# Feed-forward of a two-model kernel on Trainium2: gate, up and down as seven products of half blocks in place of eight

## The chip, the cores and the metric

The kernel runs on one core of a Trainium2 chip. The metric is the device time of one execution in microseconds (us); the median of three runs is given. The engines are TensorE (PE, with its weight loads shown as PEld), VectorE (DVE), ScalarE (ACT), GpSimd (POOL) and SyncE (SP), which issues every DMA of this kernel from one queue in program order.

## The reference, cut to what matters

The kernel computes a block with attention branches and a feed-forward, and then a second model of two layers. The change is in the first block's feed-forward alone. x1 is 1024 tokens by 1024 features, D_FF is 2816:

```python
h2 = rms_norm(x, norm_ffn[l])
x = x + (jax.nn.silu(h2 @ w_ffn_gate[l]) * (h2 @ w_ffn_up[l])) @ w_ffn_down[l]
```

Everything is float32. Each operand of a product is split into a high part (rounded to the type that TensorE takes) and a low part (the rest), and each product is three matmuls: high by high, high by low, low by high.

## The kernel before, in words

`build` first writes one list, `work`, of operations; then each engine walks the whole list in order and does what is its own. So the order in which the helpers emit operations is the order of every engine's queue. Each instruction waits for semaphores with `wait_ge`; an engine that waits holds all that stands behind.

PSUM has eight banks of 128x512. `DB` hands out six in turn for products, `TB` two (5 and 6) for the transposes of rows (`row_T`). A `Place` is one use of a bank: its `before` is that the last use has been read, `full` that the matmuls are done, `read` that it has been read. The operations that matter:

- `mm3` (L2108): for each block of 128 in the contracted dimension three matmuls of 128x128 by 128x512; before them it waits for `place.before`, for the weights' split and for its operands.
- `w_split` (L2209 on ACT makes the high part, L2371 on DVE the low part): weights come from DRAM in chunks of 1 MB into two raw buffers and are split into two double buffers.
- `row_T` (L2114, L2218, L2448): PE transposes four blocks of 128x128 into a bank of TB, ACT writes the high part, DVE the low part and frees the bank.
- `row_sq` (L2213, ACT), two short GpSimd operations (L2692, L2695) and `row_scale` (L2443, DVE): the norm of a tile of 128 rows.

The stage before the feed-forward, `row_tiles`, makes x1 from the output projection: for rows t = 0 to 3, then 4 to 7, first the left then the right half of the columns. After each product of a right half the generator `norm_row(t)` is queued, and each `tick()` moves all queued generators one step: square, scale, transpose.

The feed-forward runs over 22 strips of 128 hidden features in parts of 2, 4, 4, 4, 4 and 4 strips (`FFN_PARTS`). `f_half` makes one strip for half of the tokens:

```python
mm3(r.gate, r.gate.ps[:, :], views(ch.part(0), slice(0, 128)), views(hpair, cut), 8, ch.split, h_at[4 * hf + 3])
tick()
r.up = DB.take()
m = mm3(r.up, r.up.ps[:, :], views(ch.part(1), slice(0, 128)), views(hpair, cut), 8, ch.split)
...
emit("silu", r)
```

`silu` is a tanh on ACT (L2303), a multiply each with the gate and up banks on DVE (L2584, L2587), and the split of the strip (L2307 on ACT, L2590 on DVE). After each part the down product adds its strips: for each of two halves of the columns and each of eight row tiles one `mm3` over the part's strips, and one DVE addition into x1 in SBUF (L2579). The strips never leave SBUF. The last part goes through `row_tiles` again with `x2_row`, which stores the finished row to DRAM and transposes it for the second model's first products, one row per tick. These `row_T` write with a stride (`unmix`). GpSimd has no work of size in the stage.

Of the kernel before, what the change touches and what calls it, by code (L numbers as in the profile page):

```python
# [36 lines left out]
FFN_PARTS = (2, 4, 4, 4, 4, 4)  # L37
# [4 lines left out]
def weight_plan():  # L42
# [39 lines left out]
    f0 = 0  # L82
    for nf in FFN_PARTS:
        for f in range(f0, f0 + nf):
            add(("w_ffn_gate", 0, 8, [(f * 128, 128)]), ("w_ffn_up", 0, 8, [(f * 128, 128)]))
        for c in range(2):
            add(("w_ffn_down", f0 * 128, nf, [(512 * c, 512)]))
        f0 += nf
# [24 lines left out]
    return plan, extra  # L113
# [96 lines left out]
def build(nc, d):  # L210
    plan, extra = weight_plan()
# [6 lines left out]
    with ctx:  # L218
# [80 lines left out]
        w_todo, w_eager = [], [False]  # L299

        def w_load():
            i = ws["loaded"]
            if i >= len(plan):
# [11 lines left out]
        def w_split():  # L315
            i = ws["split"]
            if i >= len(plan) or (i in extra and not extra_bufs[extra[i]]):
                return
# [25 lines left out]
            if w_eager[0]:  # L344
                w_pump(i)

# [62 lines left out]
        def mm3(place, out, lhs, rhs, nk, split, *operands, last=True, blocks=None, start=True, stop=True):  # L409
# [7 lines left out]
            r.split, r.operands = split, flat(*operands)  # L417
            emit("mm3", r)
            w_pump()
            return place.full  # L420
# [38 lines left out]
        def row_T(src, t, ready, dst=None, unmix=False):  # L459
# [7 lines left out]
            for q0 in range(0, nk, 4):  # L467
# [4 lines left out]
                r.hi_done = signal("turned_hi")  # L472
# [858 lines left out]
        t_x1 = {t: load(f"xb{t}", x1[:, t, :], mixed_rows(d["x"], t), osp, gm["branch"]) for t in range(8)}  # L1331
# [9 lines left out]
        def row_tiles(chunks, lhs, blocks, add, finish, by_block=False, eager=True, first=False):  # L1341
# [22 lines left out]
            for t0 in (0, 4):  # L1364
                for j in range(2):
# [22 lines left out]
                    if t0:  # L1388
                        for ch in chs():
                            ch.done(m)  # L1390
            w_eager[0] = False
# [17 lines left out]
        xsf = [rest(f"xsf{i}", [T], F, (36 + 4 * i) * KB) for i in range(2)]  # L1409
        sqf = rest("sqf", [T], F, 44 * KB)  # L1410
        t_gbf = load("gbf", gbf[:, :], d["norm_ffn_b"], mix_read)
        x1_done, h_at = dict(t_x1), {}
        xsf_free = [None, None]

        def norm_row(t):
            r = Rec()
            r.src, r.junk, r.ss, r.n, r.loaded = x1[:, t, :], sqf[:, :], stat(1), T, flat(x1_done[t], mix_read)
            row_sq(r)
            yield
            r.out, r.gain, r.free = xsf[t % 2][:, :], gbf[:, :], flat(t_gbf, xsf_free[t % 2])  # L1420
            row_scale(r)
            yield
            p = row_T(xsf[t % 2][:, :], t, r.scaled)
            h_at[t], xsf_free[t % 2] = p.read, p.full

        x_last = row_tiles(chunks, lambda t: views(hpair, sl(t * 128, 128)),
                           lambda t: [(k, mix_rows[k, t // 4]) for k in range(8)], add_rows("x1"), norm_row, True)

        strips = Slots([(rest(f"fhi{i}", [T], R, 8 * i * KB), rest(f"flo{i}", [T], R, (8 * i + 4) * KB)) for i in range(6)])
        for i in range(4):  # L1430
            strips.free[i] = [x_last]

        def f_half(ch, strip, f_free, hf, made):

            fh, fl = strip
            r = Rec()
            cut = slice(hf * 512, hf * 512 + 512)
            r.gate = DB.take()
            mm3(r.gate, r.gate.ps[:, :], views(ch.part(0), slice(0, 128)), views(hpair, cut), 8, ch.split, h_at[4 * hf + 3])
            tick()  # L1440
            r.up = DB.take()
            m = mm3(r.up, r.up.ps[:, :], views(ch.part(1), slice(0, 128)), views(hpair, cut), 8, ch.split)
            tick()
            r.f_free = f_free
            r.si, r.t, r.t_free = scr.take()
            r.tanh, r.hi_done, r.lo_done = signal("f_tanh"), signal("f_hi"), signal("f_lo")
            r.hi, r.lo = fh[:, cut], fl[:, cut]
            emit("silu", r)
            scr.free[r.si] = [r.lo_done]
            made.append(r.lo_done)  # L1450
            return m

        f0 = 0
        for nf in FFN_PARTS:
            got = []
            if f0 == 0:
                chs, taken, made = [Chunk(), Chunk()], [strips.take(), strips.take()], [[], []]
                for hf in range(2):
                    for f in range(2):
                        m2 = f_half(chs[f], taken[f][1], taken[f][2], hf, made[f])  # L1460
                        if hf:
                            chs[f].done(m2)
                got = [(taken[f][0], *taken[f][1], made[f]) for f in range(2)]
                for i in range(4, 6):
                    strips.free[i] = flat(h_at[7], xsf_free)
            else:
                for f in range(nf):
                    ch = Chunk()
                    fi, pair, f_free = strips.take()
                    made = []  # L1470
                    for hf in range(2):
                        m2 = f_half(ch, pair, f_free, hf, made)
                    ch.done(m2)
                    got.append((fi, *pair, made))
            last_h = m2
            lhs_h, lhs_l = [g[1] for g in got], [g[2] for g in got]

            def rows_of(t):
                cut, hs_, ls_ = sl(t * 128, 128), lhs_h, lhs_l
                return (lambda k: hs_[k][:, cut]), (lambda k: ls_[k][:, cut])  # L1480

            def strips_of(t, got=got):
                return [(k, g[3][t // 4]) for k, g in enumerate(got)]

            f0 += nf
            if f0 < 22:
                add = add_rows("ffn")
                for c in range(2):
                    ch = Chunk()
                    for t in range(8):  # L1490
                        p = DB.take()
                        m = mm3(p, p.ps[:, :], rows_of(t), views(ch.part(0), slice(0, 512)), nf, ch.split, blocks=strips_of(t))
                        add(t, c, p)
                    ch.done(m)
                for g in got:
                    strips.free[g[0]] = [m]
                if f0 == 18:
                    m2r = rest("m2r", [8, 256], F, 32 * KB)
                    t_m2 = load("mem2", m2r[:, :, :], d["mem2T"], m)
                continue  # L1500

            x2_st, x2_last = {}, {}

            def x2_row(t):
                x2_st[t] = store("x2", mixed_rows(d["x2"], t), x1[:, t, :], x1_done[t])
                yield
                p = row_T(x1[:, t, :], t, x1_done[t], unmix=True)
                h_at[t], x2_last[t] = p.read, p.full

            m2l = rest("m2l", [8, 256], R, 32 * KB)  # L1510
            m2h = rest("m2h", [8, 256], R, 40 * KB)
            m2_hi, m2_lo = signal("m2_hi"), signal("m2_lo")
            emit("m2_split")
            pairs_ = [[Chunk()], [Chunk()]]
            m = row_tiles([lambda: pairs_[0], lambda: pairs_[1]], rows_of, strips_of, add_rows("ffn"), x2_row)
        ffn_done = m
# [6 lines left out]
        def x2_free():  # L1523
            return flat(x2_st[7], list(x2_last.values()))

        for l in range(2):
            ch = Chunk()
            for s in range(2):
# [3 lines left out]
                evac(p, [(kv[l][:, 0, s, :], p.ps[:, 0:256])], x2_free())  # L1532
# [22 lines left out]
        scr_free = flat(scr.free)  # L1555
# [356 lines left out]
        t_rx2 = {t: load(f"x2b{t}", x1b[:, t, :], d["x2"][t * 128:(t + 1) * 128, :], x2_free(), c_dead) for t in range(8)}  # L1912
# [140 lines left out]
        def h1_back(t, *dead):  # L2053
            t_rh1[t] = load(f"h1b{t}", x1b[:, t, :], d["h1"][:, t, :], h1_st[7], mem_dead, *dead)
# [17 lines left out]
        while pend:  # L2072
# [3 lines left out]
                                                   ("out", "h1", "x2", "kv1", "outB"))] + t_outC + t_outA  # L2076
# [20 lines left out]
        def _(e):  # L2097
            w = Waits(e, None)

            def mm3_run(r):  # L2100
# [3 lines left out]
                for k, made in r.blocks:  # L2104
                    if made:
                        w.wait_ge(*made)
                    for a, b in ((lh(k), rh(k)), (lh(k), rl(k)), (ll(k), rh(k))):
                        x = e.matmul(r.out, a, b, start=(r.start and m == 0), stop=(r.stop and m == n - 1))  # L2108
# [8 lines left out]
            for kind, r in work:  # L2117
                if kind == "mm3":
# [4 lines left out]
                    if r.last:  # L2123
                        x.then_inc(r.place.full[0], 1)
                elif kind == "row_T":
# [76 lines left out]
        def _(e):  # L2202
            w = Waits(e, semaphore("act_step"))
            for kind, r in work:
# [9 lines left out]
                elif kind == "row_T":  # L2214
                    w.wait_ge(*w.last)
                    w.wait_ge(*r.place.full)
                    pv = r.place.ps[:, 0:r.nb * 128].rearrange("p (k c) -> p k c", k=r.nb)
# [569 lines left out]
```

## Time and profile before

| | before |
|---|---|
| median of 3 runs (lowest, highest) | 3192.62 us (3191.34, 3193.46) |
| span of the profiled execution | 3191.1 us; the profile gives no other time for it, the runs' median is 1.5 us above its span |
| PE, DVE, ACT, POOL busy in the span | 99%, 47%, 38%, 18% |
| feed-forward stage | about 1500 to 2220 us of the span |
| mean granted clock of PE | 0.998 |

How to read it: a busy share is the time in which at least one instruction of the engine ran. A matmul's row shows its whole passage (0.39 us for 128x512), which overlaps the next one; distances between starts tell how fast they go. A granted clock of 1.00 is TensorE's 2.4 GHz, 0.50 is 1.2 GHz. "x2" in a row is two instructions in a row whose time is given together; brackets hold the idle time before and what ended it.

### The profile page before, as it was taken

What the parts mean: (1) busy time and instruction counts of PE and PEld (TensorE: products, weight loads), DVE (VectorE), ACT (ScalarE), POOL (GpSimd) and SP (SyncE); (2) the same over time, 40 slices, a digit from 0 to 9 for tenths busy, and PEclk for the clock granted to TensorE, in tenths of its full rate; (3) what the DMA queues carried; (4) which work ended last, traced back from release to release, by engine and by line L of the source; (5) the groups of instructions that cost most, each with busy time, mean ns of one, the idle gap of its engine ahead of it and who ended that gap; (6) DMA issues with size and microseconds to landing.
All of it is one profiled execution on the core that took longest, in us unless ns stands there. A gap on an engine that the chain in (4) does not pass through costs nothing.

```text
span 3191.1 us, 49353 instructions
## 1 busy us (share of the span) xinstructions
PE 3143.4 (99%) x18948; PEld 2674.9 (84%) x18948; DVE 1513.3 (47%) x3186; ACT 1215.6 (38%) x2410; POOL 565.1 (18%) x818
## 2 busy tenths in 40 slices
PE   7999999999999999999999999999999999999999
PEld 7988889999999888888888888888977777687777
DVE  6657673343354233344432333335344565753775
ACT  5446565444444122132111121124433555622452
POOL 3423334353450000000000000000101110022141
PEclk9999999999999999999999999999999999999999
DMA  5010101111113121130111111113210000212012
GB/s 202 34 47 21 34 21 47 48 54 51 44 51 103 51 75 50 50 139 14 66 42 52 53 40 53 53 53 111 77 36 27 15 28 14 97 57 89 27 60 100
DMA packets 48315, 182.44 MB, mean 57 GB/s; under 512 B 14480, under 2 KB 18704, under 8 KB 35280
## 3 DMA queue, kind: packets, MB, share of 16 engines
q1 hardware_dynamic: 48080, 179.28, 16.2%
q8 instruction: 151, 2.47, 0.3%
q14 instruction: 84, 0.69, 0.1%
HBM read 159.54 MB, written 19.46 MB: 56 GB/s over the span
## 4 chain that ended last, share of the span: by engine, by line
PE 94%; DVE 3%; ACT 2%; issue 1%; DMA 0%; POOL 0%; DVEq 0%; SPq 0%; POOLq 0%; ACTq 0%
PE ps L2108 75%; PE ps L2148 7%; PE ps L2156 3%; PE ps L2114 2%; PE ps L2163 2%; PE ps L2179 2%; PE ps L2171 1%; PE ps L2182 1%; PE ps L2199 1%; DVE wlo L2371 0%; DVE qk L2479 0%; DVE xsc L2443 0%; DVE mPT L2524 0%; DVE mE L2493 0%; DMA min<-in_mem 0%
## 5 line engine op out<-in xcount | busy, mean ns | idle before, releaser
L2108 PE MATMUL ps<-hhi,whi 128*128 128x512 f32 x1568 | 616.4, 393 | 0.0
L2108 PE MATMUL ps<-hhi,wlo 128*128 128x512 f32 x1568 | 610.9, 390 | 0.0
L2108 PE MATMUL ps<-hlo,whi 128*128 128x512 f32 x1568 | 610.1, 389 | 0.0
L2108 PE MATMUL ps<-whi,hhi 128*128 128x256 f32 (+2 forms) x1920 | 580.4, 302 | 1.3 <-DVE hlo L2573 0.9
L2108 PE MATMUL ps<-whi,hlo 128*128 128x256 f32 (+2 forms) x1920 | 563.7, 294 | 0.0
L2108 PE MATMUL ps<-wlo,hhi 128*128 128x256 f32 (+2 forms) x1920 | 563.5, 293 | 0.0
L2692 POOL TENSOR_SCALAR stats<-stats 128x2 f32<-128x2 f32 (+2 forms) x230 | 60.4, 263 | 1937.9 <-ACT jk L2213 805.0
L2108 PEld LDWEIGHTS ps<-whi,hhi 128*128 128x128 f32 x1920 | 368.3, 192 | 10.9 <-issue 3.2
L2108 PEld LDWEIGHTS ps<-wlo,hhi 128*128 128x128 f32 x1920 | 368.8, 192 | 7.6 <-issue 0.2
L2108 PEld LDWEIGHTS ps<-whi,hlo 128*128 128x128 f32 x1920 | 368.3, 192 | 7.7
L2108 PEld LDWEIGHTS ps<-hhi,wlo 128*128 128x128 f32 x1568 | 294.3, 188 | 62.1
L2108 PEld LDWEIGHTS ps<-hhi,whi 128*128 128x128 f32 x1568 | 294.5, 188 | 59.6 <-issue 0.7
L2108 PEld LDWEIGHTS ps<-hlo,whi 128*128 128x128 f32 x1568 | 294.6, 188 | 59.2
L2209 ACT ACTIVATE whi<-raw 128x1024 fp32r<-128x1024 f32 (+2 forms) x154 | 150.8, 979 | 291.8 <-PE ps L2108 286.9
L2371 DVE TENSOR_TENSOR wlo<-raw,whi 128x1024 fp32r<-128x1024 f32 (+2 forms) x154 | 173.0, 1123 | 166.7 <-ACT whi L2209 164.2
L2685 POOL CAST whi<-raw 128x512 fp32r<-128x512 f32 (+4 forms) x172 | 108.7, 632 | 649.9 <-PE ps L2108 640.5
L2687 POOL TENSOR_TENSOR wlo<-raw,whi 128x512 fp32r<-128x512 f32 (+4 forms) x172 | 219.2, 1274 | 13.8
L2695 POOL TENSOR_TENSOR stats<-stats 128x2 f32<-128x2 f32 (+2 forms) x230 | 165.6, 720 | 19.2
L2579 DVE TENSOR_TENSOR x<-ps,x 128x512 f32<-128x512 f32 x112 | 77.4, 691 | 160.5 <-PE ps L2108 159.5
L2108 PE MATMUL ps<-whi,fhi 128*128 128x512 f32 x352 | 137.5, 391 | 0.0
L2108 PE MATMUL ps<-whi,flo 128*128 128x512 f32 x352 | 137.0, 389 | 0.0
L2108 PE MATMUL ps<-wlo,fhi 128*128 128x512 f32 x352 | 136.9, 389 | 0.0
(351 smaller groups left out, 5198.5 us busy)
## 6 DMA issues: line engine op xcount, KB each, us to landing
raw<-in_W SPq DMA_DIRECT2D x93, 1024.0 KB, 4.9
raw<-in_W SPq DMA_DIRECT2D x24, 768.0 KB, 4.4
orw<-scratch_outs SPq DMA_DIRECT2D x6, 1024.0 KB, 5.4
xin<-in_x SPq DMA_DIRECT2D x8, 512.0 KB, 10.9
bW<-scratch_bw SPq DMA_DIRECT2D x8, 512.0 KB, 3.7
x<-in_x SPq DMA_DIRECT2D x8, 512.0 KB, 7.3
scratch_x<-x SPq DMA_DIRECT2D x8, 512.0 KB, 3.7
x1b<-scratch_x SPq DMA_DIRECT2D x8, 512.0 KB, 7.4
```

The source lines that it names most:

```text
L2108: x = e.matmul(r.out, a, b, start=(r.start and m == 0), stop=(r.stop and m == n - 1))
L2114: x = e.transpose(place.ps[0:rows, j * 128:(j + 1) * 128], b, ident[:, :])
L2148: x = e.matmul(p.place.ps[:, o:o + n], *p.blocks[b], start=True, stop=True)
L2156: x = e.transpose(r.place.ps[0:n, j * 128:(j + 1) * 128], r.u.E[:, o:o + n], ident[:, :])
L2163: x = e.matmul(r.v_place.ps[:, 0:r.ew], r.PT[:, j * 128:(j + 1) * 128], r.V[j], start=(j == 0), stop=(j == r.nblk - 1))
L2179: x = e.matmul(r.v_place.ps[64 * s:64 * s + 64, 0:128], u.V[j], u.PT[:, j * 128:(j + 1) * 128], start=(j == 0), stop=(j == r.nblk - 1))
L2209: e.activation(r.hi, r.raw, ACT.Copy).then_inc(w.sig(r.hi_done), 1)
L2371: e.tensor_tensor(r.lo, src, r.hi.bitcast(F), ALU.subtract).then_inc(w.sig(r.lo_done), 1)
L2579: e.tensor_tensor(r.o, r.place.ps[:, :], r.o, ALU.add).then_inc(w.sig(r.place.read), 1)
L2685: e.tensor_copy(r.hi, r.raw).then_inc(w.inner(), 1)
L2687: e.tensor_tensor(r.lo, r.raw, r.hi.bitcast(F), ALU.subtract).then_inc(w.sig(r.lo_done), 1)
L2695: e.tensor_tensor(r.ss, r.ss, half_neg[:, 0:n], ALU.pow).then_inc(w.sig(r.rstd), 1)
```

## The change: what it does

All three products become products of 2x2 blocks made with seven block products and sums of blocks (Winograd's form), where the plain form has eight.

- **Gate and up.** Activations h are cut into feature halves by token halves. Products use b11 (features low, tokens early), b21, b22 and the sums t1 to t4. The norm's late rows therefore make differences and sums with the early rows (DVE `combine`) and transpose five groups of four blocks. The weights of strips k and k + 11 with gate and up each give four half blocks of 128x512; `WeightSet` loads them (1 MB), makes four sums on GpSimd and splits seven operands on ACT and DVE. There are two sets; while one strip is computed, the next is loaded, summed and split.
- **Each of 22 strips** is seven products of 12 matmuls in the order p1, p6, p2, p7, p5, p4, p3 over four banks; p2, p4 and p3 continue a bank that an earlier product filled and that has been read in between (`joined`).
- **Finished strips.** After each odd strip GpSimd makes four sums of the outputs, and seven blocks per pair are stored to DRAM (`fs`).
- **Down** runs at the end as seven products of 11 steps; a step reads one stored strip (256 KB) and one weight block (256 KB), splits both (sums of weight blocks on GpSimd in products 2 to 5), and does 12 matmuls into four banks, three to a bank. Each product's banks are added to 1 to 4 targets of x1 (`down_add`). x1 itself is stored to DRAM before the norm and read back.
- The other weight stream is held back (`held`) from the output projection to step 40 of down. x2 rows 4 to 7 are finished during the last product, rows 0 to 3 after it, all four in the same ticks.

The diff, cut to its core:

```diff
+FF_PAIRS = 11
+FF_FIRST = ("b11", "b21", "b22", "t4", "t1", "t2", "t3")
+FF_WEIGHT = (0, 1, 6, 3, 4, 5, 2)
+FF_DOWN = ((0, "11", (0, 1, 2, 3)), (1, "21", (0,)), (4, "t1", (1, 3)), (2, "t3", (2, 3)), (5, "t2", (1, 2, 3)),
+           (3, "t4", (2,)), (6, "22", (1,)))
...
+            def load(self, i):
+                free = flat(self.raw_free() if i < 2 else self.done[:4])
+                self.landed = load(f"wf{self.x}", self.raw4[:, :, :], d["WF"][i], free)
+            def sums(self, i):
+                free = [flat(self.sums_free()) if i < 2 else flat(self.done[j]) for j in (4, 5, 6)]
+                a11, a12, a21, a22, s1, s2, s4 = self.raw
+                sum1 = combine(True, s1, a21, a22, ALU.add, self.landed, free[0])
+                sum3 = combine(True, a21, a11, a21, ALU.subtract)
+                sum2 = combine(True, s2, s1, a11, ALU.subtract, free[1])
+                sum4 = combine(True, s4, a12, s2, ALU.subtract, free[2])
+                self.ready = [self.landed, self.landed, sum3, self.landed, sum1, sum2, sum4]
+                self.after = [sum2, sum4, sum3, sum1, sum2, sum4, sum4]
...
+            # norm_row, rows 4 to 7
+            one = combine(False, h_diff[u % 2][:, :], xs[:, early], x0[:, early], ALU.subtract, hd_free[u % 2])
+            three = combine(False, xs[:, early], xs[:, late], xs[:, early], ALU.subtract)
             yield
+            p = row_T(xs[:, late], t, r.scaled, [w[:, 4:8, :] for w in hpair])
+            q = row_T(h_diff[u % 2][:, :], t, one)
+            s = row_T(xs[:, early], u, three, (t3h, t3l))
+            two = combine(False, x0[:, early], xs[:, early], x0[:, early], ALU.add, row_full[u])
+            four = combine(False, x0[:, late], x0[:, late], x0[:, early], ALU.subtract)
...
+            def keep(self):   # after p1, on ACT
+                evac(self.m1, [(self.x, self.m1.ps[:, :])], fX_free[self.i % 2])
+            def p6(self):
+                p = product(self.i, 6, self.b.take())
+                ff_add(self.x, p, self.x)
+            def u3(self):
+                ff_add(fU, self.m7, self.x)
+            def c22(self):
+                ff_add(fU, self.m5, fU)
+            def c21(self):
+                ff_add(fV, self.m4, self.x)
+                ff_out(self.i, 0, fV)
+            def p3(self):
+                self.m3 = product(self.i, 3, self.d.take(), joined=True)
+            def end(self):
+                i, k = self.i, self.i // 2
+                c12 = ff_add(self.x, self.m3, self.x)
+                fX_free[i % 2] = ff_gate(1, self.x, c12)
+                ff_out(i, 1, fU)
+                if i % 2 == 0:
+                    fo_free[0] = [fs_store(0, k, fo_made[0])]
+                    return
+                # four combine(True, ...) on GpSimd, then six stores:
+                #   fs_store(1), (3), (4, sum1), (2, sum3), (5, sum2), (6, sum4)
...
+        for i in range(2, last_strip + 1):
+            s, here, other = Strips(i), sets[i % 2], sets[1 - i % 2]
+            more = i < last_strip
+            if more:
+                other.load(i + 1)
+                other.sums(i + 1)
+            s.p1()
+            s.keep()
+            here.split(i, 6)
+            s.p6()
+            s.p2()
+            s.p7()
+            s.gate_early()
+            s.p5()
+            s.u3()
+            if more:
+                other.split(i + 1, 0, 5)
+            s.p4()
+            s.c22()
+            if more:
+                other.split(i + 1, 1, 2)
+            s.p3()
+            s.c21()
+            if more:
+                other.split(i + 1, 4, 3)
+            s.end()
...
+        for s, (p, k) in enumerate(steps):
+            strip_load(s + 4)
+            down_load()
+            if s % 3 and x1_order:
+                x1_back(x1_order.pop(0))
+            prepare(s + 2)
+            if k == 0:
+                places = [bank[4 * (p % 2) + n].take() for n in range(4)]
+            # four mm3 of one block each, then:
+            if before and k < 4:
+                down_add(p - 1, before, k)
+            if s == 40:
+                w_release(f1_last)
+            if s in (50, 56):
+                w_split()
...
+        for n in range(4):
+            down_add(6, before, n)
+            pend.append(x2_row(n))
+        tick()
```

On DVE a split's low part waits for its high part and for the sums in `after`, since it overwrites the raw block. Around `p2`, in the last strip, the first eleven down weights and four strips are read, and steps 0 and 1 are prepared in the place of the next strip's splits. In the custom order of strips 0 and 1 the same methods are called one by one. `between` (in `row_tiles`) issues set 1's sums and six splits between the left and right halves of rows 4 to 7.

## Rows read from the trace of the kernel before

**Rows 1.** The page: busy shares, and the chain that ended last.

```profile
PE 3143.4 (99%) x18948; PEld 2674.9 (84%) x18948; DVE 1513.3 (47%) x3186; ACT 1215.6 (38%) x2410; POOL 565.1 (18%) x818
...
PE 94%; DVE 3%; ACT 2%; issue 1%; DMA 0%; POOL 0%; DVEq 0%; SPq 0%; POOLq 0%; ACTq 0%
```

**Rows 2.** Windows: length, busy and count (PE, PEld, DVE, ACT, POOL), clock, DMA share, GB/s.

```profile
1440.00:1480.00 40.00, 40.00 (x190) 33.34 (x189) 15.98 (x19) 9.87 (x16) 3.67 (x6) 1.00 0.05 14
...
1600.00:2000.00 400.00, 400.00 (x1766) 331.24 (x1765) 129.88 (x161) 70.50 (x87) 0.00 (x0) 1.00 0.14 48
```

**Rows 3.** Timeline of PE: start, duration; groups of three matmuls, then eight transposes.

```profile
1376.46 0.39 PE L2108 MATMUL ps<-hlo,whi 128*128 128x512 f32 x1
1376.69 0.39 PE L2108 MATMUL ps<-hhi,wlo 128*128 128x512 f32 x1
1376.92 0.39 PE L2108 MATMUL ps<-hhi,whi 128*128 128x512 f32 x1
...
1457.87 1.03 PE L2114 MATMUL ps<-ident,xsf 128*128 128x128 f32 x8
1458.66 0.48 PE L2108 MATMUL ps<-whi,hhi 128*128 128x512 f32 x1
```

**Rows 4.** Groups by line and shape, 1440 to 2240 us: busy us, mean ns, idle before.

```profile
L2579 DVE TENSOR_TENSOR x<-ps,x 128x512 f32<-128x512 f32 x105 | 72.6, 691 | 143.4 <-PE ps L2108 142.5
L2590 DVE SCALAR_TENSOR_TENSOR flo<-scr,fhi 128x512 fp32r<-128x512 f32 x44 | 30.4, 692 | 36.5 <-ACT fhi L2307 36.5
...
L2443 DVE SCALAR_TENSOR_TENSOR xsf<-x,stats,gbf 128x1024 f32<-128x1024 f32 x7 | 9.0, 1284 | 0.2
...
L2307 ACT ACTIVATE fhi<-scr 128x512 fp32r<-128x512 f32 x44 | 27.8, 633 | 243.9 <-DVE scr L2587 243.9
```

**Rows 5.** Timeline of POOL with DVE quiet on SBUF: copy, then difference.

```profile
2901.59 0.61 POOL L2685 CAST whi<-raw 128x512 fp32r<-128x512 f32 x1
2902.28 1.28 POOL L2687 TENSOR_TENSOR wlo<-raw,whi 128x512 fp32r<-128x512 f32 x1
```

**Rows 6.** DMA issues: KB each, median us from issue to landing.

```profile
raw<-in_W SPq DMA_DIRECT2D x93, 1024.0 KB, 4.9
...
tabM<-in_tabM SPq DMA_DIRECT2D x1, 256.0 KB, 2.6
```

**Rows 7.** Timelines of POOL and DVE, both on SBUF at once.

```profile
63.04 2.13 POOL L2687 TENSOR_TENSOR wlo<-raw,whi 128x512 fp32r<-128x512 f32 x1
...
62.52 1.51 DVE L2443 SCALAR_TENSOR_TENSOR xsc<-xin,stats,gb 128x1024 f32<-128x1024 f32 x1
```

**Rows 8.** PE's timeline before, at and after an idle of 1.84 us.

```profile
330.76 0.28 PE L2108 MATMUL ps<-wlo,hhi 128*128 128x256 f32 x1
330.88 0.28 PE L2108 MATMUL ps<-whi,hlo 128*128 128x256 f32 x1
333.01 0.41 PE L2114 MATMUL ps<-ident,qk 128*128 128x128 f32 x2 [1.84 <-DVE qk L2479]
...
335.44 0.41 PE L2108 MATMUL ps<-whi,hhi 128*128 128x256 f32 x1
335.65 0.41 PE L2108 MATMUL ps<-wlo,hhi 128*128 128x256 f32 x1
```

**Rows 9.** Windows: the clock is third from last, GB/s last.

```profile
20.00:30.00 10.00, 9.36 (x79) 9.16 (x78) 5.87 (x9) 5.26 (x8) 3.61 (x7) 1.00 0.99 405
30.00:40.00 10.00, 6.85 (x36) 6.28 (x36) 7.11 (x11) 7.21 (x13) 3.22 (x5) 0.67 0.33 107
...
336.00:337.00 1.00, 1.00 (x7) 1.00 (x6) 0.00 (x0) 0.00 (x0) 0.00 (x0) 0.50 0.98 410
337.00:338.00 1.00, 1.00 (x9) 0.84 (x10) 0.00 (x0) 0.19 (x1) 0.00 (x0) 0.94 0.99 418
```

**Rows 10.** Timeline: the splits of one row tile turned with a stride.

```profile
2212.31 2.19 ACT L2218 ACTIVATE hhi<-ps 128x512 fp32r<-128x512 f32 x2 [3.70 <-PE ps L2114]
2213.49 2.19 DVE L2448 TENSOR_TENSOR hlo<-ps,hhi 128x512 fp32r<-128x512 f32 x2 [0.92 <-ACT hhi L2218]
```

More of the change, by code:

```diff
@@ L81, in weight_plan @@
         add(("w_out", c % 2 * 512, 4, [(c // 2 * 512, 512)]))
[L82 to L88, printed above, removed]
+    held = len(plan)
     for l in range(2):
@@ L407, in split_half, with mm3 @@
             return r.lo_done
-        def mm3(place, out, lhs, rhs, nk, split, *operands, last=True, blocks=None, start=True, stop=True):
+        def mm3(place, out, lhs, rhs, nk, split, *operands, last=True, blocks=None, start=True, stop=True, joined=False, step=None):
             r = Rec()
@@ L1339, in four_chunks, with row_tiles @@
             return [lambda: pair(0), lambda: pair(1)]
-        def row_tiles(chunks, lhs, blocks, add, finish, by_block=False, eager=True, first=False):
+        def row_tiles(chunks, lhs, blocks, add, finish, by_block=False, eager=True, first=False, between=None):
             w_eager[0] = eager
@@ L1390, in row_tiles @@
                             ch.done(m)
+                        if between and not j:
+                            between()
             w_eager[0] = False
@@ L1430, in build @@
[L1430 to L1435, printed above, removed]
-            r = Rec()
[L1437 to L1465, printed above, removed]
-            else:
[L1467 to L1515, printed above, removed]
@@ new lines, in turn_t4, with first_weights @@
+        def turn_t4(u):
+            p = row_T(x1[:, u, late], u, late_ops[u][1], (t4h, t4l), free=[[x1_kept[t] for t in range(4, 8)], late_ops[3][1]])
+            h_read["t4"].append(p.read)
+            return p.full
+        def first_weights():
+            sets[1].sums(1)
+            sets[0].split(0, 0, 1, 2, 4)
+            sets[1].split(1, 0, 1)
+        for i in range(2):
+            sets[i].load(i)
+        sets[0].sums(0)
+        x_last = row_tiles(chunks, lambda t: views(hpair, sl(t * 128, 128)),
+                           lambda t: [(k, mix_rows[k, t // 4]) for k in range(8)], add_rows("x1"), norm_row, True, between=first_weights)
@@ new lines, in product, with ff_add @@
+        def product(i, p, place, joined=False):
+            s, j, name = sets[i % 2], FF_WEIGHT[p - 1], FF_FIRST[p - 1]
+            lhs = [(lambda k, w=w: w[:, 128 * k:128 * k + 128]) for w in (s.hi[j], s.lo[j])]
+            s.done[j] = mm3(place, place.ps[:, :], lhs, h_ops[name], 4, s.made[j], h_read[name], start=not joined, joined=joined)
+            return place
+        def ff_add(out, place, other):
+            r = Rec()
+            r.out, r.place, r.other = out, place, other
+            emit("ff_add", r)
+            return place.read
@@ new lines, in build @@
+        s0, s1 = Strips(0), Strips(1)
+        s0.p1()
+        tick()
+        fX_free[:] = [row_scaled[7], row_scaled[7]]
+        s0.keep()
+        s1.p1()
+        s1.keep()
+        for u in range(3):
+            turn_t2(u)
+        s0.p2()
+        tick()
+        assert not pend
+        fT_free[:] = [flat(xsf_free[0]), flat(xsf_free[0])]
+        sets[0].split(0, 5, 3, 6)
+        s1.p2()
+        turn_t2(3)
+        t4_full = [turn_t4(u) for u in range(4)]
+        for j in range(7):
+            fo_free[j] = flat(h_read["t2"], h_read["t4"], t4_full, [x1_kept[t] for t in range(4)])
@@ new lines, in build @@
+        s0.gate_early()
+        s0.p7()
+        s0.p5()
+        s0.p6()
+        sets[1].split(1, 2, 4, 5)
+        s1.p7()
+        s0.u3()
+        s0.p4()
+        s0.c22()
+        sets[0].load(2)
+        sets[1].split(1, 3, 6)
+        s0.p3()
+        sets[0].sums(2)
+        s0.c21()
+        s0.end()
+        s1.gate_early()
+        s1.p6()
+        s1.p5()
+        s1.u3()
+        sets[0].split(2, 0, 5)
+        s1.p4()
+        s1.c22()
+        sets[0].split(2, 1, 2)
+        s1.p3()
@@ new lines, in build, with x2_row, down_add @@
+        f1_last = s.m3.full
+        x2_st, x2_last = {}, {}
+        def x2_row(t):
+            x2_st[t] = store("x2a" if t > 3 else "x2b", mixed_rows(d["x2"], t), x1[:, t, :], x1_done[t])
+            yield
+            p = row_T(x1[:, t, :], t, x1_done[t], unmix=True)
+            h_at[t], x2_last[t] = p.read, p.full
+        def down_add(p, places, n):
+            r = Rec()
+            r.place, r.outs = places[n], []
+            for target in FF_DOWN[p][2]:
+                t, c = 4 * (target // 2) + n, target % 2
+                r.outs.append((x1[:, t, c * 512:c * 512 + 512], t_x1[t]))
+                x1_done[t] = places[n].read
+            emit("down_add", r)
```

347 lines of the change are left out of this document (302 added, 45 removed).

## The prediction

> **What bounds the kernel now.** The page first: TensorE (PE) is busy 99% of the span and carries 94% of the chain that ended last [rows 1]. Then the windows over the feed-forward stage: PE is busy without a gap at full clock in each, and from 1600 to 2000 us 1766 matmuls start in 400 us, 0.2265 us each [rows 2]. The duration of 0.39 us on a matmul's row overlaps the next; the starts count. The timeline shows 0.227 us between starts for groups of three matmuls that change PSUM bank each time too, the form of the new down product [rows 3]. So a matmul removed here is worth 0.2266 us, and every wait of PE is new time: none lies there now. VectorE (DVE) is busy a third of this stage, so counts of work hide nothing; what must be read is who waits for whom.
>
> **Matmuls removed.** Before: 22 strips x (gate + up) x 8 blocks x 2 halves x 3 = 2112, and 22 x 8 x 2 x 3 = 1056 down. After: 22 strips x 7 products x 4 x 3 = 1848, and 77 steps x 12 = 924. 396 fewer x 0.2266 = **-89.7 us**.
>
> **Transposes added.** Rows 0 to 3 turn 8 blocks of 128x128 each as before; with each late row come five groups of four (b22, t1, t3, t2, t4) instead of two: 32 + 80 = 112 blocks where 64 were. Eight take 0.79 us from start to the next matmul [rows 3]: 48 x 0.1 = **+4.8**.
>
> **Start of the stage, DVE's queue.** Each late row turns three blocks of four in a row, and only two banks (5, 6) serve row_T. The third waits until the first is split: ACT 0.63, DVE 0.69, handoffs of 0.2, less the 0.4 of the neighbour's transposes: 1.1 us x 4 = 4.4. DVE does per late row one add, a scale of 1.28, four combines of 0.69, three lows of 0.69 [rows 4]: 6.8 us, against 24 matmuls (5.44) and 1.2 of transposes on PE; the six weight splits issued at `between` make it some 4 us late already, so row 6 is turned 1 us late, the third t2 block (behind row 7's scale and combines) 2.2 us, the five t2/t4 blocks (behind three weight lows) 2.3. In strips 0 and 1, u3 stands behind three lows, c22 behind a low that waits for strip 2's sums: 1.0 + 1.2. Together **+12** (bounds 3, the bank waits alone being in part covered, to 25, if DVE runs at the speed it has beside GpSimd, below).
>
> **Strips 2 to 21, the term that decides.** One product is 12 x 0.2266 = 2.72 us, a strip 19.04; p3 should start at 16.3. It continues bank d, so it waits for c22's read; c22 stands in DVE's queue behind the lows of operands 0 and 5 of the *next* strip; low 5 waits for that strip's sum4 on GpSimd. Follow an even strip, zero at its start. The odd strip before it ends with c12, tanh, gate, output: 0.69 + 0.63 + 0.69 + 0.69 and handoffs [rows 4], 3.0. Then four sums of GpSimd, 1.28 + 0.07 each [rows 5], 8.4. SyncE (SP) is held by the six stores of those sums, which stand before the next load: issue about 8.8. 1 MB lands 4.9 later [rows 6]: 13.7. Four more sums: 19.1. Low 5 and c22: 20.6. p3 starts 4.3 us late. Beside DVE work on two SBUF operands a GpSimd op took 2.13 instead of 1.28 us and DVE's own 1.51 for 1.28 [rows 7]; low 6 falls into the first four sums, so I add 0.3 and take 4.6. An odd strip has no wait: the strip before it makes no sums at its end, its one store is ready, the load goes at 0.4 and sum4 ends near 11. Strips 2, 4, ... 20: 10 x 4.6 = **+46** (bounds 3.9 and 6.5 each: 39 to 65). That GpSimd shares its SBUF interfaces with DVE when DVE has two SBUF inputs is what the Trainium skill says (GPSIMD Engine Reference, Specifications); the rows agree, 2.13 against 1.28.
>
> **The clock after these waits.** PE idles 1.84 us before 333.01; after it resumes, starts are 0.21 us apart in place of 0.12 [rows 8], and the granted clock is 0.50 until 337.0, 0.94 in the next us [rows 9]: taken from where it fell, 333.6, some 3.4 us at 1.2 GHz, 1.7 us lost, then 2.4 GHz again. (Of 30 to 40 us a mean of 0.67 is some 6.7 us at 1.2 GHz, twice that.) A wait of 4.6 us is far longer, so I give each such loss once: 10 x 1.7 = **+17** (bounds 0, and 34 from the longer case), and once each for the waits in the down product and at the end: **+3.4**. The Trainium skill (TensorE: Matmul & The Clock Gate, HAM oscillation) says that waits repeated in a loop make each next group start cold. By that rule the sum stands; without it, it is 20 us lower, a rival below.
>
> **Down product, 77 steps of 2.72 us.** ACT has two splits (1.3), DVE two lows (1.4), GpSimd one sum in four of the seven products (1.3): all fit, and prepare(s+2) has two steps, 5.4 us, for a chain of 2.7 to 3. What doesn't fit: (a) in strip 21, c22 behind the lows of step 0, whose strip is read only when p7 frees the slot: 0.3. (b) strip_load(4) stands on SP behind the last stores (8.5 us in), lands 2.6 later [rows 6], is split by 13.3 where step 4 is due at 10.9: 2.4. (c) four adds per bank after product 0: DVE has 4.15 us of work in steps of 2.72, four times, slack 3.3: 2.4. (d) three adds per bank at steps 55 to 58 with sums on GpSimd beside them and a weight chunk's lows (2048 columns, under four times 0.69) at 56: 3. Sum **+8** (bounds 3 and 30, below). Traffic: steps 0 to 11 read 10.2 MB (strips, weights, x1) in about 30 us, 313 GB/s; 405 was reached with rows of 4 KB and more [rows 9]; here most rows are 2 KB, which no row shows under load.
>
> **End.** x2 rows 0 to 3 are turned in one burst: 8 blocks of four through two banks. With the scattered destination ACT and DVE take 1.1 us each per block [rows 10]: a bank returns after 2.8 us, so 9.9 us for 3.2 of PE: **+6.7** (bounds 3, the burst overlapping kv products, to 8). Before, row by row under products, this cost nothing.
>
> **Hidden.** A strip's other work lies under its 19 us of PE: on DVE 7 lows, 5 additions, 2 gates and 2 outputs, 16 x 0.69 = 11 us; on ACT 7 splits, 2 tanh and a copy, 10 x 0.63 = 6.3; on GpSimd 6 sums in the mean, 8.1. Only their order costs, above. The stores and x1's trip to DRAM run on idle queues; the later W chunks are loaded from step 40 on, 36 steps before use.
>
> **Sum.** -89.7 + 4.8 + 12 + 46 + 17 + 3.4 + 8 + 6.7 = **+8.2 us** on the span of 3191.1. Around the span lie 1.5 us (median 3192.6 of the runs shown): **3201 us**. 0.2%, 6.4 us, is about what this kernel's measurement can tell.
>
> **Rivals.**
> 1. *The clock holds.* Waits cost only themselves: 3201 - 20 = 3181. For it: from 20 to 30 us PE paused for 0.64 us and the clock stayed at 1.00 [rows 9]. Against: 1.84 us sufficed at 333 us [rows 8].
> 2. *No wait in the even strips* (other side, faster). The price is that of one place: p3 behind sum4. It vanishes if sum4 ends by 14.8 instead of 19.1, which needs the load out before the stores, or GpSimd sums at some 0.7 us, DVE's price. Then 3201 - 63 = 3138. Decision point: wait and clock together cost 6.3 per even strip here; below 4.8 the kernel is faster by over 0.2%. Against: the order on SP and GpSimd is fixed in the code, and each link has a row.
> 3. *Down product bound by reads or DVE.* If 2 KB rows move at half of 405 GB/s, 10.2 MB take 51 us instead of some 33: +18; with DVE lows at the contended price in products 2 to 5, another 5 to 10: 3220 to 3230. For: SP waits in order, so one late strip delays the rest. Against: 256 KB landed in 2.6 us.
>
> **Chances.** Forecast 0.50 (own range 3188 to 3222: slower 0.35, same 0.13, faster 0.02), rival 1 0.20 (faster 0.16, same 0.04), rival 2 0.15, rival 3 0.15 (slower). Together faster 0.33, same 0.17, slower 0.50. The range 3150 to 3230 takes in forecast, rival 1 and most of rival 3, and leaves out rival 2 and a tail above.
>
> **What would show it.** PE matmuls of the stage: 2772 of 128x512. In strips 2 to 20, waits of PE for DVE (c22's line, the ff_add) of about 4.6 us, ten times, and none of size in odd strips; a granted clock below 1.00 right behind each. GpSimd's sums at 1.3 us in two bursts of four per even strip. PE waiting for DVE lows in the down product near steps 4 and 13 to 16, and at row_T at the stage's two ends. Wrong if the ten waits are absent or above 6.5 us; if the clock stays at 1.00; if the down product's steps take 3 us or more throughout.

## The result and the profile after

The changed kernel takes **3262.2 us** (median of 4, 3261.5 to 3266.4) against 3192.8: a ratio of 1.022, 95% interval 1.021 to 1.024. It is 69 us slower. The prediction was 3201 us, with a range up to 3230: the direction was its likelier one, the size and the range were wrong. The profiled execution has a span of 3259.7 us (before 3191.1).

The page after, busy shares and the chain that ended last, beside [rows 1]:

```profile
PE 3104.6 (95%) x18600; PEld 2629.8 (81%) x18600; DVE 1740.3 (53%) x3480; ACT 1332.9 (41%) x2640; POOL 811.5 (25%) x994
...
PE 32%; DVE 4%; ACT 1%; DMA 1%; issue 1%; POOL 0%; SPq 0%; DVEq 0%; POOLq 0%; ACTq 0%
```

PE has 348 instructions fewer than in [rows 1] (396 matmuls gone, 48 transposes come), but is busy only 39 us less, since rows at half clock last longer. The chain's shares add up to 39%: it was followed back only to about 1986 us, so its 32% for PE does not compare with the 94% before. The windows of the stage, in the columns of [rows 2]:

```profile
1500.00:1600.00 100.00, 83.33 (x348) 66.67 (x349) 55.22 (x76) 31.47 (x52) 22.78 (x18) 0.90 0.15 53
1600.00:2000.00 400.00, 348.24 (x1453) 284.17 (x1452) 208.98 (x278) 107.54 (x172) 139.54 (x104) 0.94 0.24 86
2000.00:2300.00 300.00, 267.47 (x1187) 217.32 (x1186) 217.86 (x251) 127.91 (x187) 72.91 (x48) 0.95 0.47 159
```

In the 400 us from 1600, where 1766 matmuls started before, 1453 do: 52 us without work, and a clock of 0.94 for 1.00. Up to about 1485 us the two traces agree within 1 us, and from the end of the stage on the trace after is 67 to 69 us behind: all but about 2 us happen inside the stage. What PE waited for, whole run (us in total, times, longest):

```profile
PE ps L2470 <- DVE fU L2960: 62.6, 12, 6.5
PE ps L2477 <- DVE hlo L2816: 10.3, 11, 1.9
PE ps L2470 <- DVE fb1l L2739: 7.3, 4, 3.7
PE ps L2470 <- DVE x L2974: 7.0, 1, 7.0
```

One line carries most: p3, which continues bank d, waits for c22, the DVE addition that reads this bank (`fU`, L2960). Ten of those twelve waits are in the even strips 2 to 20, 57.2 us, none in an odd strip of the loop before strip 21. One of them is shown here in the timelines of SP, POOL, DVE and PE. It lies in strip 4, whose first matmul starts at 1607.34:

```profile
1606.33 10.68 SPq L2454 DMA_DIRECT2D scratch_fs<-fo  x6
1617.17 0.33 SPq L2451 DMA_DIRECT2D wf<-in_WF  x1
...
1610.94 5.72 POOL L3075 TENSOR_TENSOR fo<-fo,fo 128x512 f32<-128x512 f32 x4 [13.68 <-DVE fo L2968]
1622.04 1.29 POOL L3075 TENSOR_TENSOR wf1s<-wf 128x512 f32<-128x512 f32 x1 [5.38 <-issue]
...
1626.09 1.27 POOL L3075 TENSOR_TENSOR wf1s<-wf,wf1s 128x512 f32<-128x512 f32 x1
...
1626.15 1.76 DVE L2739 TENSOR_TENSOR wf1l<-wf,wf1h 128x512 fp32r<-128x512 f32 x1 [6.97 <-POOL wf1s L3075]
1627.94 0.69 DVE L2739 TENSOR_TENSOR wf1sl<-wf1s,wf1h 128x512 fp32r<-128x512 f32 x1
1628.67 0.69 DVE L2960 TENSOR_TENSOR fU<-ps,fU 128x512 f32<-128x512 f32 x1
...
1629.41 0.80 PE L2470 MATMUL ps<-hhi,wf0h 128*128 128x512 f32 x1 [5.60 <-DVE fU L2960]
1630.01 0.63 PE L2470 MATMUL ps<-hlo,wf0h 128*128 128x512 f32 x1
...
1632.55 0.39 PE L2470 MATMUL ps<-hlo,wf0h 128*128 128x512 f32 x1
```

Read it downwards: the output of the odd strip before is there, four sums run on POOL (1610.94 to 1616.66), SP holds the next load behind their six stores until 1617.17, the megabyte lands at 1622.0, four more sums, then the low of operand 0, which is written over the raw block and so waited for the third of those sums; it took 1.76 us beside the fourth, where a low alone takes 0.69. Then the low of operand 5, then c22. The matmuls behind the wait start 0.43 us apart instead of 0.227 for 3 us. The granted clock there, third column from the end, is 0.50 (1.2 GHz), then 1.00 (2.4 GHz):

```profile
1630.00:1631.00 1.00, 1.00 (x4) 0.81 (x3) 0.93 (x3) 0.00 (x0) 0.00 (x0) 0.50 0.00 0
...
1632.00:1633.00 1.00, 1.00 (x4) 0.76 (x4) 0.96 (x2) 0.00 (x0) 0.00 (x0) 0.74 0.00 0
1633.00:1634.00 1.00, 1.00 (x6) 0.81 (x5) 0.72 (x2) 0.00 (x0) 0.00 (x0) 1.00 1.01 344
```

### The profile page after: what moved, and what is told of

Same layout as the page of the kernel before. It is cut to its first block and busy times, and to the rows that moved or that the text cites. A ratio compares the mean times of both kernels' runs of the same rounds, so it can differ in the third digit from the quotient of the medians.

```text
span 3259.7 us, 50403 instructions
## 1 busy us (share of the span) xinstructions
PE 3104.6 (95%) x18600; PEld 2629.8 (81%) x18600; DVE 1740.3 (53%) x3480; ACT 1332.9 (41%) x2640; POOL 811.5 (25%) x994
## 5 line engine op out<-in xcount | busy, mean ns | idle before, releaser
L2470 PE MATMUL ps<-hhi,whi 128*128 128x512 f32 x864 | 342.6, 397 | 0.0
L2470 PE MATMUL ps<-hhi,wlo 128*128 128x512 f32 x864 | 337.3, 390 | 0.0
L2470 PE MATMUL ps<-hlo,whi 128*128 128x512 f32 x864 | 336.6, 390 | 0.0
L2470 PEld LDWEIGHTS ps<-hhi,wlo 128*128 128x128 f32 x864 | 162.3, 188 | 34.6
L2470 PEld LDWEIGHTS ps<-hhi,whi 128*128 128x128 f32 x864 | 162.5, 188 | 32.0 <-issue 0.7
L2470 PEld LDWEIGHTS ps<-hlo,whi 128*128 128x128 f32 x864 | 162.6, 188 | 31.9
L2739 DVE TENSOR_TENSOR wlo<-raw,whi 128x768 fp32r<-128x768 f32 (+2 forms) x86 | 92.8, 1079 | 153.8 <-ACT whi L2574 152.5
L2470 PE MATMUL ps<-hhi,wf0h 128*128 128x512 f32 x176 | 78.8, 448 | 57.2 <-DVE fU L2960 57.2
L2574 ACT ACTIVATE whi<-raw 128x768 fp32r<-128x768 f32 (+2 forms) x86 | 80.3, 934 | 105.1 <-PE ps L2470 102.3
L2513 PE MATMUL ps<-mkT,mqT 96*128 96x512 f32 (+3 forms) x288 | 117.0, 492 | 0.9 <-DVE stats L2861 0.5
```

Source lines behind the costliest of these rows:

```text
L2513: x = e.matmul(p.place.ps[:, o:o + n], *p.blocks[b], start=True, stop=True)
L2574: e.activation(r.hi, r.raw, ACT.Copy).then_inc(w.sig(r.hi_done), 1)
L2739: e.tensor_tensor(r.lo, src, r.hi.bitcast(F), ALU.subtract).then_inc(w.sig(r.lo_done), 1)
```

## The experiments

Every time below stands beside the kernel before on the same chip (3192.2 to 3192.8 us). "The kernel after" is the changed kernel, 3262.2.

**1. c22 first.** c22 goes ahead of the next strip's lows in DVE's queue:

```diff
-            if more:
-                other.split(i + 1, 0, 5)
-            else:
-                prepare(0)
             s.p4()
             s.c22()
+            if more:
+                other.split(i + 1, 0, 5)
+            else:
+                prepare(0)
```

> In strips 2 to 21 the addition c22 is emitted ahead of the next strip's first two splits; the same work, in another order on DVE. Theory A (p3 waits for c22, which stands on DVE behind low 5, which waits for sum4; the clock then falls): the ten waits of 5.5 to 6.5 us and that of 3.3 in strip 21 vanish, and with them the low clock behind them; strips 2 to 21 lose 81 us less, so 3262 - 81 - 3 = about 3178. Rival B (the chain of loads and GpSimd sums is itself too long for the strip, so that the wait only moves to the next strip's p1 or p6, which need low 0 and low 5): the time falls by less than half of that, above 3220, and PE waits for a low of a weight operand.

Measured: 3224.7 us, ratio 1.010 (1.009 to 1.012). It gains 37 us, less than half of the 84 us that the expectation put on these waits and the clock behind them: rival B. The ten waits for c22 are gone; in their place the next odd strip's first product waits, ten times, mostly for the low of operand 0 (30.0 us in 11 waits for it, after 1.7 in one). Timelines of POOL, DVE and PE:

```profile
1623.12 1.27 POOL L3075 TENSOR_TENSOR wf1s<-wf,wf1s 128x512 f32<-128x512 f32 x1
...
1623.17 1.76 DVE L2739 TENSOR_TENSOR wf1l<-wf,wf1h 128x512 fp32r<-128x512 f32 x1 [5.46 <-POOL wf1s L3075]
...
1625.09 0.77 PE L2470 MATMUL ps<-hhi,wf1h 128*128 128x512 f32 x1 [2.73 <-DVE wf1l L2739]
```

So the order on DVE was only half of it: the chain of output, stores, load and sums ends later (20.0 us into strip 4 of the kernel after) than the strip does (19.04 without a wait), and whoever is last in line waits for it.

**2. Load before stores.** The load of strip i+2's weights is issued at the end of strip i's products, ahead of the odd strip's stores on SP (strip 3's load stays where it was):

```diff
             if more:
-                other.load(i + 1)
+                if i % 2 or i == 2:
+                    other.load(i + 1)
                 other.sums(i + 1)
...
+            if i % 2 and i + 2 <= last_strip:
+                here.load(i + 2)
             s.end()
```

> The load of strip i+2 is issued ahead of the six stores that end odd strip i instead of behind them (from strip 4 on); DVE's order is as in the changed kernel. Theory A: SP held by the stores is a link of the chain; with the load out, sum4 of even strips ends near 14 us instead of 20, so low 5 and c22 are done about 16 and p3 waits under 1 us; nine of ten waits go: 3262 - 9 x 8.1 = about 3189. Rival C (GpSimd alone is the link, its eight sums beside DVE's work being longer than the strip allows): half of the waits stays, 3220 or more.

Measured: 3197.8 us (ten runs, 3192.4 to 3199.1), ratio 1.001 (1.001 to 1.002): 64 us gained by where the loads of nine strips stand in SP's queue. The expectation's 3189 was too low by 9: the nine waits did not vanish but left 3.8 us, strip 2's grew by 1.5, and the rest was not traced. Timelines of SP, POOL and PE of the same strip:

```profile
1606.22 0.33 SPq L2454 DMA_DIRECT2D wf<-in_WF  x1
1607.68 21.07 SPq L2457 DMA_DIRECT2D scratch_fs<-fo  x7
...
1618.11 1.29 POOL L3078 TENSOR_TENSOR wf1s<-wf 128x512 f32<-128x512 f32 x1
...
1625.56 0.50 PE L2473 MATMUL ps<-hhi,wf0h 128*128 128x512 f32 x1 [0.39 <-DVE fU L2963]
```

The weight sums now follow the output sums without a pause: they begin 9.4 us into the strip instead of 14.7. Strip 2 still waits 7.0, the other nine even strips 0.4 to 0.7 each, at nearly full clock.

**3. Useless matmuls in the wait.** The kernel after, with 24 matmuls more into a free bank ahead of p3 in every even strip from 2 to 20; nothing that p3 waits for is changed:

```diff
+            if more and i % 2 == 0:
+                emit("pe_fill", r)
             s.p3()
...
+                    for m in range(r.n):
+                        e.matmul(r.ps[:, :], r.lhs[:, 128 * (m % 4):128 * (m % 4) + 128], r.rhs(m % 4), start=True, stop=True)
```

> Before p3 of the even strips 2 to 20, PE runs 24 matmuls more (5.4 us) into a bank that the next strip overwrites; their result is used by nobody. Nothing else changes, so p3 starts no earlier. Theory of the clock (the idle of 5.6 us lets the granted clock fall, which costs 2.4 us more per even strip): the clock stays at 1.00 in these strips and 240 matmuls more make the kernel FASTER by about 24 us, near 3238. Rival (the low clock is not due to the idle, or PE's reads delay DVE): no gain or a loss, 3262 or above.

Measured: 3244.0 us, ratio 1.016 (1.015 to 1.018). With 240 matmuls *more* the kernel is 18 us faster. This shows the clock's part of the loss in these ten strips apart from the waits, and as a lower bound: p3 starts 22.4 us into the strip in the mean, 22.2 in the kernel after, so 2 us went the other way. The 3238 of the expectation was too low by 6. PE's timeline, the filling and p3's first matmul, and a window for the clock (1.00, where the kernel after has 0.94):

```profile
1623.35 5.60 PE L2499 MATMUL ps<-t4h,wf0h 128*128 128x512 f32 x24
1629.37 0.50 PE L2476 MATMUL ps<-hhi,wf0h 128*128 128x512 f32 x1 [0.42 <-DVE fU L2970]
```

```profile
1600.00:1900.00 300.00, 296.19 (x1298) 242.88 (x1297) 161.45 (x217) 82.39 (x132) 105.69 (x80) 1.00 0.25 89
```

c22 in strip 4 is done as late as it was (1629.3, and 1629.4 in the kernel after); only the matmuls behind it are quick at once.

**4. The memory rows' split earlier.** At the end of the stage PE waits 7.0 us at the first product of memory rows, for the last additions, which stand on DVE behind `m2_split`. That split is issued two steps before the end of the down product:

```diff
+            if s == len(steps) - 3:
+                m2_free[:] = [b_made[len(steps) - 1]]
...
+                emit("m2_split")
```

> The split of mem_2 is emitted two steps before the end of the down product, ahead of the last row_T and of the last additions. Theory D (the 7.0 us that PE waits after the seven products are due to DVE's last additions and mem_2's low part standing behind ACT's split of mem_2, which stands behind the last row_T): the wait falls below 1 us, the clock stays up behind it, 3262 - 6 - 2 = about 3254. Rival (the four additions, or the banks, are late by themselves): 3260 or more.

Measured: 3262.1 us, no gain. The wait itself fell from 7.0 to 3.3 us:

```profile
2273.95 0.39 PE L2471 MATMUL ps<-m2h,whi 128*128 128x256 f32 x1 [3.26 <-DVE x L2975]
```

What is left are the last late row's strided splits, which stand ahead of the additions too. From the first matmul of the down product to the end, this profile is 3.6 us shorter than that of the kernel after (1227.4 for 1231.1); before it, the even strips and the start of the stage, which the edit does not touch, happened to wait 3.7 us more. So the size of the gain stays open; the edit is used again below.

**5. The down product's sums on DVE.** The 44 sums of the down product's weights move from GpSimd to DVE (`combine(True, ...)` to `combine(False, ...)` in `prepare`):

> Only change to the kernel after: the 44 weight sums of the down stage go from GpSimd to VectorE, so GpSimd is idle there. Theory A, contention: the five waits for a weight low between 2134 and 2149 us (1.24 to 1.75 each, 8.1 in all) stand because the lows take 1.66 us beside the sums on GpSimd and about 0.7 when it is idle; with the sums on VectorE at 0.7 (low and sum 1.4 together instead of 1.66) these waits go, and the time is 3250 to 3255. Rival B, work: VectorE is simply full in the down stage, and 44 more operations of it make it later; the waits for lows grow and the time is 3265 or more.

Measured: 3264.5 us, ratio 1.022 (1.021 to 1.024): no gain, as rival B expected, though the waits of theory A are gone. The kernel after, timelines of POOL, DVE and PE in product t3, and the window:

```profile
2132.35 9.44 POOL L3075 TENSOR_TENSOR wd<-wd,wd 128x512 f32<-128x512 f32 x6
...
2134.62 1.42 DVE L2974 TENSOR_TENSOR x<-ps,x 128x512 f32<-128x512 f32 x2
...
2137.63 1.64 DVE L2739 TENSOR_TENSOR fb0l<-wd,fb0h 128x512 fp32r<-128x512 f32 x1
...
2139.33 0.51 PE L2470 MATMUL ps<-fb0h,fa1h 128*128 128x512 f32 x1 [1.70 <-DVE fb0l L2739]
```

```profile
2120.00:2160.00 40.00, 34.57 (x147) 26.97 (x146) 38.23 (x33) 15.86 (x26) 33.51 (x22) 1.00 0.40 130
```

and with the sums on DVE, the same window and two rows:

```profile
2120.00:2160.00 40.00, 39.68 (x176) 32.53 (x175) 35.80 (x52) 17.46 (x28) 0.00 (x0) 1.00 0.50 174
```

```profile
2134.26 0.69 DVE L2951 TENSOR_TENSOR wd<-wd,wd 128x512 f32<-128x512 f32 x1
...
2135.78 0.69 DVE L2739 TENSOR_TENSOR fb0l<-wd,fb0h 128x512 fp32r<-128x512 f32 x1
```

The contention is real: DVE does 52 operations in less busy time than 33 before, and 29 more matmuls start in 40 us. The waits that it removes are four, 5.4 us in all (2134.6 to 2148.8); the expectation said five and 8.1, counting in two at 2080 and 2085, which stay here at 1.23 and 1.40 and so are no contention. But the down product as a whole takes 236 us from its first matmul to its last in both: at steps 56 to 61, where a weight chunk's lows (2.5 us) and three additions per bank meet the sums, PE now waits 6.8 us in place of 4.7, 4.35 of it at once, and the clock falls there (0.97 in the 60 us from 2160). The gain of one place was given back in the next.

**6. All edits, with and without c22 first.** The early load (now for strip 3 too, ahead of strip 1's stores), the sums on DVE, `m2_split` early, `strip_load(4)` issued with the first four, and the last late row turned behind the last additions; then the same with c22 first.

```diff
-                for n in range(4):
+                for n in range(5):
                     strip_load(n)
...
-            elif p == 6 and k % 2 == 0:
+            elif p == 6 and k % 2 == 0 and k < 10:
...
             pend.append(x2_row(n))
+        next(rows_late.pop(0), None)
         tick()
```

> The same six edits less the move of c22. Theory A, the waits are separate: 3168 to 3176, below the kernel before by 16 to 24. Rival B: the waits at strip 2, in the down stage and at the end move on to the next instruction when they are taken away where they stand (as that at the end did when the split of the memory rows alone was moved), and the time stays within 5 of the 3198 of the early load alone.

> Six edits to the kernel after: the weights of strip i+2 loaded ahead of the seven stores of the odd strips, and the load of strip 3 so too; c22 emitted ahead of the next strip's lows; the down stage's sums on VectorE; the fifth strip load of the down stage with the first four; the split of the memory rows two steps earlier; and the last late row turned behind the last additions. Theory A: each wait has its own cause and the gains add: from 3198 of the load alone 9 less at strip 2, 10 at the sums, 5 at step 4, 5 to 8 at the end, and 3 to 5 from the c22 waits of 0.4 to 0.7 that were left: 3163 to 3172. Rival B: with c22 ahead the next odd strip waits for its first low instead, as when c22 alone was moved, and this kernel is 5 or more slower than the same without that edit.

Measured: without c22 first 3182.5 us (ratio 0.997, 0.996 to 0.998), with it **3171.5 us** (0.993, 0.992 to 0.995). The first missed its forecast by 6.5, the second is inside; c22 first is worth 11 us once the chain is short, where 3 to 5 were expected, and no odd strip waits any more.

**7. Order alone, and one split moved.** First, the early load and c22 first and nothing else; second, all edits with the second weight split moved from step 56 of the down product to step 61.

```diff
-            if s in (50, 56):
+            if s in (50, 61):
```

> Only two things of order are changed in the kernel after: the weight loads of strips 3 and up go ahead of the stores of the odd strips on the DMA queue, and c22 goes ahead of the next strip's lows. Theory A, two separate delays on one chain: the early load takes the GpSimd sums some 5 us forward, so that the low for the next strip's first product is made in time although c22 goes first, and no strip waits: from 3198 with the early load alone about 9 less at strip 2 and 5 for the waits of 0.4 to 0.7, so 3182 to 3187, and PE busy throughout from 1560 to 1920 with the clock at 1.00. Rival B: the early load has already taken all that c22 held, the move of c22 then gives nothing or costs a wait for the first low of each odd strip, and the time is 3190 or more.

> The kernel with all six edits (3171.5), and the second of the two weight splits inside the down stage moved from step 56 to step 61, behind the steps in which the three-fold additions of the product before stand on VectorE. Theory A: the wait of 4.34 us at step 57 (2123.7) is the sum of that split (2.5 us) and the additions (2.1 per step), and goes: 3165 to 3168. Rival B: VectorE is so full there (18 of 20 us) that the split costs the same wait wherever it stands: 3170 to 3173.

Measured: order alone **3178.0 us**, ratio 0.996 (0.994 to 0.997), 84 us below the kernel after and 14 below the one before, and 4 below the forecast's range. A window of it, and the same of the kernel after:

```profile
1600.00:1900.00 300.00, 300.00 (x1326) 248.47 (x1325) 180.89 (x251) 100.16 (x160) 126.75 (x96) 1.00 0.29 103
```

```profile
1600.00:1900.00 300.00, 265.06 (x1111) 216.61 (x1110) 155.47 (x209) 79.38 (x127) 102.97 (x77) 0.94 0.24 88
```

Not one matmul waits in strips 2 to 21, and the clock stays at 1.00. The second: 3168.0 us (0.9925, 0.991 to 0.994), the fastest of all. Against the 3171.5, measured on another chip, the intervals overlap, so the 3.4 us are not shown. The wait of 4.34 is gone, but two of 1.4 came in its place (idle at steps 58 to 65 6.8, now 5.9), so DVE's fullness there is probably the larger part. PE's timeline in the kernel with all edits, and in this one:

```profile
2123.73 0.66 PE L2477 MATMUL ps<-fb0h,fa0h 128*128 128x512 f32 x1 [4.34 <-DVE fb0l L2746]
```

```profile
2126.64 0.50 PE L2477 MATMUL ps<-fb0h,fa0h 128*128 128x512 f32 x1 [1.43 <-DVE fb0l L2746]
```

## Why the prediction was wrong

The sum said +8.2 on the span, +68.6 was measured: 60 us were missed. Its terms (us), with waits and distances between starts summed from PE's timeline from 1480 to 2310:

| term | predicted | measured |
|---|---|---|
| matmuls, transposes | -89.7 + 4.8 | 348 instructions fewer, as predicted |
| waits at the start | 12 | 14.4 |
| waits, even strips 2 to 20 | 46 | 57.2 |
| strip 21's c22, and the down product | 0.3 + 7.7 | 3.3 + 17.6 |
| waits at the end | 6.7 | 11.7 |
| clock, strips | 17 | 22.2 |
| clock, elsewhere | 3.4 | about 15 |
| overlap lost at the waits | not in the sum | 7.7 |
| left over | | 4.6 |

The waits add up to 104.2 us. The clock's 37 are counted from the matmuls that start further apart than at full speed while the granted clock is 0.50. The next line is the passage of a matmul: its row of 0.39 us overlaps the next by 0.16, and a wait counts only from the row's end, so each of 42 waits costs 0.16 or more beyond its idle time. The strips check it: strips 2 to 20 took 443.0 us, 19 times 19.04 is 361.8, and of the 81.2 between, 57.2 are waits, 1.6 lost overlap and 22.2 the clock. Of the 4.6 left over, 1.8 arise behind the stage; the price of the transposes has no check of its own.

- **No step alone explains the miss; the one that failed most is "The clock after these waits".** The mechanism held, ten of ten, and rival 1 (the clock holds) is refuted by experiment 3. The size did not: 1.5 to 3.1 us per wait, 2.2 in the mean, where 1.7 was taken from the shorter of the two cases in [rows 9]. Above all the term was charged at twelve places, and the waits of 1 to 7 us at the start of the stage, in strip 21, at step 4, and at its end cost the clock too: 0.92 from 1480 to 1560, 0.83 from 2260 and 0.74 from 2280 on. Together this is 17 of the 60 us missed; the down product's waits are 13, those of the even strips 11, those at the end 5.
- **"Strips 2 to 21": right link by link, each link short.** In strip 4 the odd strip's output was ready at 3.4 (3.0 predicted), the four output sums ended at 9.3 (8.4), the load was issued at 9.8 (8.8), landed at 14.7 (13.7), sum4 ended at 20.0 (19.1), c22 at 22.0 (20.6): a wait of 5.6 us for 4.6. Of the last 1.4, 0.9 is the longer chain, the rest the low of operand 0, which the prediction let pass in the shadow of sum4: it started beside it and took 1.76 for 0.69. The Trainium skill (SBUF — State Buffer, two separate sides) states it harder than the page of the skill that the prediction cited: the pair is an exclusive lock, held for the whole instruction, and the other engine fully blocks. The trace nearly agrees: the low, begun 0.06 us after the sum, ends 0.55 after it, where a low alone takes 0.69. By that rule the last links would have been priced at once.
- **Rival 2 had the right place and decision point, and needed both halves.** A wait-and-clock cost of 4.8 per even strip was to decide; it measured 8.1, and the kernel is slower. The early load alone (experiment 2) left small waits and strip 2's, c22 alone moved the wait to p1. Both together give 3178.0; taking 81.2 (443.0 - 361.8) from 3262.2 gives 3181.0. The 3138 of the rival started from a sum that was too low elsewhere.
- **"Down product": rival 3's half came true inside the forecast.** Its reads were no bound: 352 GB/s were moved with rows of mostly 2 KB from 2040 to 2060, and behind step 4 PE waited for nothing until 2080. Its contended DVE lows, put at 5 to 10, cost four waits, 5.4 us, between 2134 and 2149. The four places named were there, each larger: (b) 3.7 for 2.4, (c) 2.6 for 2.4, (d) 4.7 for 3, and (a) 3.3 for 0.3, since step 0's strip, issued behind eleven weight loads, landed after 5.1 us, not 2.6. Small waits make the other 1.1.
- **"End": the burst was right (4.7 of waits for 6.7), but the additions before it cost 7.0.** The sum had them at nothing. They stand on DVE behind `m2_split` and the strided lows of the last late row, and PE's next bank waits for them; no cover was named for them, and none was there. With both moved away (experiment 6) the wait is 0.14.
- **The range.** Waits of 57 and clock of 22 lay inside their own bounds, 39 to 65 and 0 to 34; with both as measured the sum is already 16 higher. The range treated terms as if they would cancel, but waits, clock and contention err to the same side: each late link also lowers the clock behind it.

## What to carry to other kernels

When a change takes work from an engine that was never idle, price the order of the queues before the work: here 396 matmuls fewer were worth 90 us, the order of one load behind six stores and of one addition behind two lows took 84 back, and both could be swapped without any other change. Moving only the instruction that is waited for moves the wait to the next in line; shorten the chain behind it first, then reorder, and look at the next stage after each edit, since a wait taken away in one product can come back in the next. Where a PE wait can't be removed, it costs itself and what the clock loses behind it, in the even strips here about 40% more (22.2 on 57.2).

## What the hardware showed that was not expected

- A DVE low with two SBUF sources (0.69 us) took 1.51 to 1.76 beside a GpSimd sum, which itself took 1.27 to 1.6; an addition with one source in PSUM kept its 0.71 in the same stretch (1.42 for two, experiment 5). [rows 7] had shown mainly GpSimd losing.
- Three waits of 1.68 to 1.72 us, 4.7 us apart (2139 to 2149), left the clock at 1.00, where 1.84 had cost it in [rows 8]; the ten of 5.5 to 6.5 cost 1.5 to 3.1 us each beyond themselves. 24 useless matmuls in each of them made the kernel 18 us faster.
- The same strip loop gave waits of 5.5 to 6.5 us for one chain of fixed length; why single strips vary by 1 us was not tried.
